# Two-layer decoder trunk on one core: the five stationary arrays are placed at other addresses within 512 bytes

## The reference

```python
h = rms_norm(x, gain);  proj = h @ w_in          # 2048 -> 6160: q, k, v, r and a low-rank gate
x = x + gated_linear_attention(proj) @ w_out     # 2048 -> 2048
x = x + (silu(g) * u) @ ffn_w_out                # g, u = rms_norm(x) @ ffn_w_in: 2048 -> 2 x 5632 -> 2048
k, v = rms_norm(x) @ w_kv                        # 2048 -> 4096, shared
x = x + diff_attention(rms_norm(x) @ w_q, k, v) @ w_out
x = x + (silu(g) * u) @ ffn_w_out                # the second SwiGLU
```

## Time and profile before

| | |
|---|---|
| median of three runs | 2254.92 us |
| the profiled execution, its own time | 2255.17 us |
| span of the core in it | 2253.4 us |
| what lies around the span | 1.8 us |
| TensorE matmul busy | 2248.0 us (100%), 9732 matmuls |
| TensorE weight load busy | 1817.1 us (81%) |
| VectorE, ScalarE, GpSimd busy | 1250.4, 1058.7, 281.0 us |
| DMA | mean 198 GB/s, 447 MB |
| granted TensorE clock | 1.0 (2.4 GHz) |

### The profile page before, as it was taken

How to read it: one execution, slowest core, us unless ns; L and a number is a source line. 1 busy time by engine, 2 the same in 40 slices (tenths; PEclk the granted TensorE clock), 3 DMA queues, 4 the chain that set the end, 5 groups by cost and what they waited for, 6 DMA issues and landing times.

```text
span 2253.4 us, 27280 instructions
## 1 busy us (share of the span) xinstructions
PE 2248.0 (100%) x9732; PEld 1817.1 (81%) x9732; DVE 1250.4 (55%) x1472; ACT 1058.7 (47%) x1432; POOL 281.0 (12%) x563
## 2 busy tenths in 40 slices
PE   9999999999999999999999999999999999999999
PEld 7888888888888888888888888888888888888887
DVE  5665666545554555454556675665555555544443
ACT  6665455444444444444455665554444444434332
POOL 3210334100000000001124333340000000000000
PEclk9999999999999999999999999999999999999999
DMA  8765667666666666666667666677666766666665
GB/s 259 203 186 172 191 191 221 194 209 196 196 201 198 203 197 200 193 195 198 198 192 214 192 203 196 197 219 205 191 206 195 206 194 198 199 206 188 187 187 160
DMA packets 252674, 447.01 MB, mean 198 GB/s; under 512 B 27664, under 2 KB 41968, under 8 KB 252592
## 3 DMA queue, kind: packets, MB, share of 16 engines
q1 hardware_dynamic: 236176, 428.79, 63.4%
q0 software_dynamic: 16240, 17.07, 2.6%
q10 hardware_dynamic: 176, 0.07, 0.0%
HBM read 414.37 MB, written 2.10 MB: 185 GB/s over the span
## 4 chain that ended last, share of the span: by engine, by line
PE 100%; DVE 0%; ACT 0%; issue 0%; POOL 0%; DVEq 0%; ACTq 0%; POOLq 0%
PE acc L654 32%; PE acc L653 32%; PE acc L655 32%; PE acc L665 1%; PE acc L670 0%; PE side L905 0%; PE tps L692 0%; PE side L717 0%; PE side L741 0%; PE side L776 0%; PE side L903 0%; PE side L920 0%; PE side L921 0%; PE side L919 0%; PE side L790 0%; PE side L791 0%
## 5 line engine op out<-in xcount | busy, mean ns | idle before, releaser
L1343 DVE TENSOR_TENSOR w_lo<-raw,w_hi 128x1024 fp32r<-128x1024 f32 x784 | 954.8, 1222 | 871.8 <-ACT w_hi L966 867.6
L966 ACT ACTIVATE w_hi<-raw 128x1024 fp32r<-128x1024 f32 x784 | 826.8, 1058 | 1050.2 <-PE acc L655 1037.1
L653 PE MATMUL acc<-w_hi,xT 128*128 128x512 f32 x2016 | 803.2, 398 | 0.0
L654 PE MATMUL acc<-w_lo,xT 128*128 128x512 f32 x2016 | 801.5, 398 | 0.0
L655 PE MATMUL acc<-w_hi,xT 128*128 128x512 f32 x2016 | 801.4, 398 | 0.0
L655 PEld LDWEIGHTS acc<-w_hi,xT 128*128 128x128 f32 x2016 | 379.5, 188 | 91.0
L654 PEld LDWEIGHTS acc<-w_lo,xT 128*128 128x128 f32 x2016 | 379.6, 188 | 90.4
L653 PEld LDWEIGHTS acc<-w_hi,xT 128*128 128x128 f32 x2016 | 379.5, 188 | 90.3
L653 PE MATMUL acc<-w_hi,hT 128*128 128x512 f32 x700 | 278.3, 398 | 0.0
L655 PE MATMUL acc<-w_hi,hT 128*128 128x512 f32 x700 | 278.3, 398 | 0.0
L654 PE MATMUL acc<-w_lo,hT 128*128 128x512 f32 x700 | 278.3, 398 | 0.0
(11 more groups left out here) (207 smaller groups left out, 1391.9 us busy)
## 6 DMA issues: line engine op xcount, KB each, us to landing
raw<-in_ffn_w_in SPq DMA_DIRECT2D x352, 512.0 KB, 4.0
raw<-in_ffn_w_out SPq DMA_DIRECT2D x176, 512.0 KB, 4.8
raw<-in_gla_w_in SPq DMA_DIRECT2D x96, 512.0 KB, 4.2
raw<-in_w_kv SPq DMA_DIRECT2D x64, 512.0 KB, 4.4
raw<-in_gla_w_out SPq DMA_DIRECT2D x32, 512.0 KB, 4.7
raw<-in_diff_w_q SPq DMA_DIRECT2D x32, 512.0 KB, 4.5
raw<-in_diff_w_out SPq DMA_DIRECT2D x32, 512.0 KB, 4.8
tok<-scratch SPq DMA_DIRECT2D x352, 32.0 KB, 3.2
```

Of the source, the lines that this page charges most:

```text
L653: nc.tensor.matmul(acc[p][tb][:, ::-1], hi, w_hi[:, slot, j, ::-1], start=(kt + j == 0), stop=False)
L654: nc.tensor.matmul(acc[p][tb][:, ::-1], hi, w_lo[:, slot, j, ::-1], start=False, stop=False)
L966: nc.scalar.activation(w_hi[:, slot, :, :], raw[:, slot, :, :], ACT.Copy).then_inc(hi_done, 1)
L1343: nc.vector.tensor_tensor(w_lo[:, slot, :, :], raw[:, slot, :, :], w_hi[:, slot, :, :].bitcast(F32), ALU.subtract).then_inc(lo_done, 1)
```

## The change

The five arrays get starts other than 0 by 512. `xT` begins at 128, `hT` at 64, `g_oT` at 192, `xT_q` at 32, `d_oT` at 96. A gap behind `xT` puts `raw` back at 0, and with it `w_hi`, `w_lo` and all that follows them. What stands behind the other four arrays follows their offset: `x_turned` (behind `hT`) begins at 64, and `q_squares`, `p_squares`, `p_turned` (behind `d_oT`) at 96. No instruction is added, removed or moved, and `unit` still reads the moving row from its end to its start.

```diff
         x = sb("x", [P, TB, D])
+        place("gap_xT", 128)
         xT = sb("xT", [P, 2, KT, S], F32R)
+        place("gap_raw", 0)
         raw = sb("raw", [P, SLOTS, UNIT_KT, CB])
...
-            place("gap_g", 0, s1)
+            place("gap_g", 192, s1)
             g_oT = sb("g_oT", [P, 2, KT, S], F32R, s1)
         with ExitStack() as s1:
-            place("gap_h", 0, s1)
+            place("gap_h", 64, s1)
             hT = sb("hT", [P, 2, FKT, S], F32R, s1)
...
-            place("gap_d", 0, s1)
+            place("gap_q", 32, s1)
             with ExitStack() as s2:
                 xT_q = sb("xT_q", [P, 2, KT, S], F32R, s2)
+            place("gap_d", 96, s1)
             d_oT = sb("d_oT", [P, 2, KT, S], F32R, s1)
```

## The result

The changed kernel takes 2268.30 us (2268.16 to 2268.57, 3 runs) against 2254.92 us: 13.4 us or 0.6% more, a ratio of 1.006 with a 95% interval of 1.0037 to 1.0082. The profiled execution took 2268.57 us, with a span of 2266.8 us.

What follows compares the result with a forecast made beforehand. It took the number of matmuls times their start-to-start interval as the bound. All terms were taken as 0, so it predicted the unchanged median, 2254.9 us (no change 0.36), with a range of 2200 to 2297 us.

Steps and rivals of the forecast that it cites:

- What bounds the kernel: Whole kernel: TensorE is never fed too slowly; time is 9300 matmuls at 233.3 ns, 2170 of 2253.4 us.
- Part (a): Hot-loop matmul interval on the five moved arrays: bounded by -86 to +62 us, taken as 0 ns.
- the gate's mean: Gate matmuls at mixed offsets: 117.5 ns each, 10.8 on top of their columns; read as no effect of placement.
- the settled step: Difference of the settled upward and downward intervals, 226.7 and 233.3 ns: 6.7 ns, worth 40.3 us on `xT`.
- C: Rival: the interval on `xT` rises one step to 240 ns, 2295.2 us, with `hT` too 2309 us; chance 0.15.
- E: Rival: intervals on `xT` no longer settle and wander, 2169 to 2271 us; chance 0.04 down, 0.03 up.
- E's far end: Hot-loop reads cease to meet at all: 216 ns per matmul, -161 us, 2094 us; given next to nothing.
- D's upper value: Rival: `xT` stays and `hT` gets slower by 14.0 us, 2269 us; chance 0.08 for this side.
- B's argument: Rival: 233.3 lies high in 224 to 240 ns, so `xT` falls one step, 2214.6 us; chance 0.28.
- 234.1: Interval in ns on `xT` above which slower was to be decided: 0.2% of the time, 4.5 us, over 6048 matmuls.
- Parts (b) to (d): First and last units (-0.3 to +1.4 us), gate's moving reads (at most 0.3 us), writers and transfers: each taken as 0.
- (e): Chain from `raw` to `w_lo`: keeps up with units of 2720 ns, so a faster interval would be kept in full.

Runs made afterwards that it cites:

- the upward run: The kernel before, all offsets 0, with the hot loop reading its moving rows and writing its results upwards: 2193.98 us, ratio 0.9732.

## Why the prediction was wrong

*What bounds the kernel* held: 9300 matmuls times their interval, with nothing else on the path. The whole change is in the interval, on `xT`, and ScalarE and VectorE wait for it about as much longer (16.6 and 15.3 us against 13.3).

*Part (a) failed.* I took 0 ns on `xT` because the gate's mean over offsets 0, 128, 256 and 384 was close to the mean at 0. Measured is +13.3 us, 2.2 ns in the mean over 6048. The error behind the number is the step before it: "then the interval settles at once" was read at distance 0, where one interval is steady in each direction, and I took for granted that another distance would have one as well, which might lie elsewhere. At 128 there are three. The gate's spread of 9 ns in the earlier trace rows, against 1 ns in the earlier trace rows, spoke against this, and I let its mean outweigh it; by itself the spread could not show several intervals at one distance, since four distances were mixed in it. The mean was a weak measure too. It was taken upwards, on 96 stationary and 256 moving columns, and compared with the hot loop by a proportion (10.0 ns of 13.3) that no row supports; and half of its tiles lay at 0 and 256, the best distances upwards. Upwards 128 costs 5.7 ns on `xT` (232.4 against 226.7), which the gate's mean did not show either. The price of the settled step, 6.7 ns, was right as an end, but there is a half step, 3.3 ns, and it made 8.4 of the 13.2 us.

*The rivals.* None of them is what happened. C had the sign and the 240.0 ns, but on all of `xT` and so 40 us; it came true on 708 of 6048 matmuls. E spoke of intervals that no longer settle and wander between the ends. Its number for 236 ns on `xT`, 2271 us, comes close, since the mean became 235.5, and its sign, 5 ns or more between the records of the group, would have been read as met (397 in one stretch, 402 in another); but the mechanism is another, because each stretch does settle, on one interval or on one short pattern, and keeps it for as long as 2112 matmuls. At E's far end I took the 216 ns of the float32 passes for next to nothing on top. They are passes of 256 columns, for which I counted 106.7 ns in the gate, so they are no measure of what 512 columns of float32r could reach. D's upper value, 2269 us, meets the measured time, but for a reason that the trace refutes: `hT` at 64 is unchanged. B's argument, that 233.3 lies high in the range and could fall, is answered by the table: downwards nothing goes below it. The mean of 235.5 ns on `xT` lies past 234.1, the point from which C was to decide, so that test pointed to the side of slower, as was measured; it couldn't tell one step on all of `xT` from a mixture.

*Parts (b) to (d) held.* The first units' interval rose by some 2.7 ns (their 96 matmuls start between 8.3 and 33.2 us, before 8.3 and 33.0), 0.3 us in all, within -0.3 to +1.4. The gate's 32 matmuls take 117.4 ns each against 117.5. The moves into `x_turned` land in 3.8 us against 3.7, beside matmuls, with TensorE never idle for them. (e) was needed for the upward run instead: at 226.7 ns TensorE still waits only at the start (1.2 and 0.8 us), and 61 of the 62 us worked out for it were kept.

*The rule of the notes.* That the weight load has its own port and takes nothing from the running matmul (the Trainium skill, TensorE: Matmul & The Clock Gate, Part 2, step 1) pointed to no change. The runs don't agree with that conclusion: with nothing altered but where the arrays lie, the interval goes from 226.7 to 234.3 ns upwards (`d_oT` from 0 to 96) and downwards from 233.3 up to 240.0 (`xT` from 0 to 128). I discounted the page's number but kept the conclusion; neither holds for these matmuls. Whether it is the port that is shared, or something else that both reads go through, no run here shows.

*Open:* that the 13 to 27 ns over 512 columns' own 213.3 come from the two reads meeting in the memory is argued from distance and direction, not shown by itself; and what at the start of a stretch picks one of the three intervals was not found. Perhaps it isn't fixed by the kernel alone: the two groups of times with `xT` alone moved, and one time of four 2.2 and 2.3 us below the median of the other three in the two runs with small matmuls added, would fit one stretch of 360 in another interval. Not all of those executions were profiled, so this isn't shown.

## What to carry to other kernels

Where a row of equal matmuls bounds the kernel, read the interval from start to start in each stretch, not the mean of a group: a mixture of steady intervals looks like a small general loss. For matmuls like these (float32r, 128 stationary and 512 moving columns, a new stationary tile each time) place the stationary tiles and the moving rows at a distance of 0 by 256 bytes and read upwards; moving both by 128 was free, moving one was not. Other shapes and types were not run. A distance at which several intervals are steady makes the time depend on harmless edits: one extra small matmul ahead of a long stretch cost 14 us here.

## What the runs showed of the hardware that was not expected

- An interval can have a memory of hundreds of microseconds: the same instructions at the same addresses ran at 233.3 or at 240.0 ns for 2112 matmuls, depending on one matmul of 128 columns ahead of them.
- The steady patterns repeat after a whole number of 6.67 ns. 226.7, 233.3 and 240.0 are 34, 35 and 36 times 6.67; 236.7 ns is the mean of an alternation of about 235 and 238.5, together 71 times. Some stretches at 233.3 are an alternation too, of 231.5 and 235. Upwards, 228.9 is a pattern of three matmuls (103 times) and 232.4 one of seven, from 228 to 241 ns, together 1626.7 ns (244 times). Where this step comes from no run shows.
- Beside a downward read at distance 0 the direction in which the results are written to PSUM costs nothing; reading the moving row downwards instead of upwards costs 6.7 ns over 226.7.
